# Two more blocks of the first projection in rounded products, and three low halves made by adding DMAs

## The reference

```python
h = _rmsnorm(x, norm_g[layer, 0]) * (1.0 + scale_m) + shift_m
proj = h @ w_in                        # (256 x 1024) @ (1024 x 3072)
a_val, a_gate, q, k, v, g = split(proj)
a = a_val * sigmoid(a_gate)            # then a convolution of 31 taps over the tokens
a = silu(layernorm(conv(a)))
r = silu(g) * head_rmsnorm(retention(rotary(q), rotary(k), v))
mix = concatenate([a, r]) @ w_out
```

## Time and profile before

| | before |
|---|---|
| median of 3 runs | 1171.31 us (1170.61 to 1175.93) |
| profiled execution, span | 1171.0 us (no other time is shown for this execution) |
| TensorE busy | 1112.6 us, 95% |
| VectorE busy | 816.0 us, 70% |
| ScalarE busy | 557.7 us, 48% |
| chain that ended last | TensorE 78%, VectorE 10%, DMA 5%, ScalarE 5% |
| mean granted TensorE clock | 0.985 of full speed |

### The profile page before, as it was taken

The page is one execution under the profiler, slowest core; times in us unless marked ns, Lnnn a source line. Parts: engine busy times, 40 slices in busy tenths (PEclk is TensorE's granted clock), DMA queues, the critical chain, the costliest instruction groups (busy, mean ns, idle before and its releaser), DMA issues.

```text
span 1171.0 us, 22089 instructions
## 1 busy us (share of the span) xinstructions
PE 1112.6 (95%) x9466; PEld 995.9 (85%) x9466; DVE 816.0 (70%) x1390; ACT 557.7 (48%) x876; POOL 44.6 (4%) x71
## 2 busy tenths in 40 slices
PE   6899898999999997879999999999999999999998
PEld 4778686988888885469999999999988899988898
DVE  1599466877578674875666654478899966659955
ACT  3224633445111124554555543356568846467944
POOL 0010001000000000000000000000000000042000
PEclk8999999999999998999999999989989999999999
DMA  9887688899848957865355555525433345343342
GB/s 369 356 280 269 250 323 315 305 339 328 335 182 258 342 186 165 323 245 184 140 184 182 183 189 185 187 81 180 145 109 114 130 153 177 131 153 117 108 145 72
DMA packets 38290, 246.46 MB, mean 210 GB/s; under 512 B 4400, under 2 KB 5584, under 8 KB 9648
## 3 DMA queue, kind: packets, MB, share of 16 engines
q1 hardware_dynamic: 29072, 182.36, 45.7%
q0 software_dynamic: 6240, 43.94, 10.0%
q10 hardware_dynamic: 2880, 18.74, 3.9%
HBM read 225.24 MB, written 19.79 MB: 209 GB/s over the span
## 4 chain that ended last, share of the span: by engine, by line
PE 78%; DVE 10%; DMA 5%; ACT 5%; issue 2%; SPq 0%; ACTq 0%; DVEq 0%
PE ps L1452 16%; PE ps L1454 15%; PE ps L1456 15%; PE ps L1459 10%; PE ps L1555 4%; DMA ca_dram<-more 2%; PE ps L1648 1%; PE ps L1528 1%; PE ps L2083 1%; PE ps L1601 1%; PE ps L1539 1%; PE ps L1534 1%; DMA more<-in_ada_w 1%; DVE ring_rounded L2229 1%; DMA ada_more<-in_ada_w 1%
## 5 line engine op out<-in xcount | busy, mean ns | idle before, releaser
L1452 PE MATMUL ps<-sq_rounded,w_high_rounded 128*128 128x256 f32 x1184 | 341.6, 288 | 2.5 <-DVE mixT_rounded L2236 1.3
L1456 PE MATMUL ps<-sq_rounded,ring_rounded 128*128 128x256 f32 x1184 | 336.2, 284 | 0.0
L2229 DVE TENSOR_TENSOR ring_rounded<-ring,w_high_rounded 128x1024 fp32r<-128x1024 f32 x220 | 260.6, 1226 | 92.1 <-ACT w_high_rounded L844 91.8
L1454 PE MATMUL ps<-hT_rounded,w_high_rounded 128*128 128x256 f32 x992 | 282.1, 284 | 0.0
L844 ACT ACTIVATE w_high_rounded<-ring 128x1024 fp32r<-128x1024 f32 x220 | 219.8, 1049 | 67.0 <-PE ps L1456 66.3
L1452 PEld LDWEIGHTS ps<-sq_rounded,w_high_rounded 128*128 128x128 f32 x1184 | 228.5, 193 | 11.0 <-issue 6.7
L1456 PEld LDWEIGHTS ps<-sq_rounded,ring_rounded 128*128 128x128 f32 x1184 | 228.6, 193 | 0.0
L1454 PEld LDWEIGHTS ps<-hT_rounded,w_high_rounded 128*128 128x128 f32 x992 | 191.8, 193 | 0.1
L1452 PE MATMUL ps<-more_rounded,w_high_rounded 128*128 128x256 f32 x448 | 127.4, 284 | 0.4 <-issue 0.3
L1456 PE MATMUL ps<-more_rounded,ring_rounded 128*128 128x256 f32 x448 | 126.8, 283 | 0.0
L1459 PE MATMUL ps<-big,ring 128*128 128x256 f32 x544 | 121.0, 381 | 0.0
(11 more groups left out here) (426 smaller groups left out, 1640.3 us busy)
## 6 DMA issues: line engine op xcount, KB each, us to landing
ring<-in_blocks SPq DMA_DIRECT2D x139, 1024.0 KB, 4.9
ada_w<-in_ada_w POOLq DMA_DIRECT2D x27, 1024.0 KB, 7.7
ada_more<-in_ada_w POOLq DMA_DIRECT2D x13, 1024.0 KB, 7.6
we_dram<-we_t ACTq DMA_DIRECT2D x8, 1024.0 KB, 8.3
ca_dram<-more ACTq DMA_DIRECT2D x8, 1024.0 KB, 11.9
ring<-we_dram SPq DMA_DIRECT2D x8, 1024.0 KB, 5.5
ring<-ca_dram SPq DMA_DIRECT2D x8, 1024.0 KB, 6.8
big<-in_ada_w SPq DMA_DIRECT2D x4, 1024.0 KB, 10.9
```

Of the source, the lines that this page charges most:

```text
L1452: nc.tensor.matmul(out, high[:, k, columns], x_high, start=start, stop=False, skip_group_check=True)
L1454: nc.tensor.matmul(out, high[:, k, columns], x_low, start=False, stop=False, skip_group_check=True)
L1456: last = nc.tensor.matmul(out, low[:, k, columns], x_high, start=False, stop=stop, skip_group_check=True)
L2229: nc.vector.tensor_tensor(rounded(w), w, w_high[:, c % 2, ks], ALU.subtract)\
```

## The change

Blocks 5 and 7 become split blocks. For them and for block 8 the low half is no longer made by VectorE. ScalarE rounds the block into `w_high` and then overwrites the ring slot with the rounded negative of the block; POOL then issues a DMA that reads the same block from DRAM again and adds it to what lies in the slot, which leaves the low half. TensorE takes the two products with the high weights for the whole block first, waits for the adding DMA, and then takes the product with the low weights. POOL issues the three adds behind pieces 10, 11 and 13 of `ada_w`. ScalarE's rounding is called at new places: block 5 behind the first sigmoid, block 7 behind the second, block 8 behind the copies of unit 4. On VectorE `centre` comes ahead of the low half of block 11. `dq_here` is folded into `lam_here` (which now counts to 32), `positions_here` and `p_here` into `small_here` (48).

```diff
-W_IN_SPLIT = (8, 9, 10, 11)
+W_IN_SPLIT = (5, 7, 8, 9, 10, 11)
+ADD_BEHIND = {10: 5, 11: 7, 13: 8}
+LOW_BY_DMA = {"w_in": (5, 7, 8)}
...
+            if b - start in LOW_BY_DMA.get(name, ()):
+                added[b] = 1 + sum(place[a] % 2 == place[b] % 2 for a in added)
+                low[b] = 0
+                continue
...
+            def add_low(name, j):
+                b = first_block[name] + j
+                pool.wait_ge(w_high_ready, 2 * split_place[b] + 2)
+                pool.dma_start(rounded(ring[:, b % RING]).rearrange("p a b -> p (a b)"), dram["blocks"][laid_out[b]],
+                               accum_op=ALU.add).then_inc(w_low_added[split_place[b] % 2], 16)
...
                 pool.dma_start(ada_slots[slot].rearrange("p a b -> p (a b)"), dram["ada_w"][n]).then_inc(ada_here[slot], 16)
+                if n in ADD_BEHIND:
+                    add_low("w_in", ADD_BEHIND[n])
...
+                    if b in low_added:
+                        nc.scalar.activation(w_high[:, c % 2], ring[:, b % RING], ACT.Copy).then_inc(w_high_ready, 1)
+                        nc.scalar.activation(rounded(ring[:, b % RING]), ring[:, b % RING], ACT.Copy, scale=-1.0)\
+                            .then_inc(w_high_ready, 1)
...
                 for n in (*pieces_at("w_in", 2 * j), *pieces_at("w_in", 2 * j + 1)):
                     modulation_row(n)
+                round_to(first_block["w_in"] + (6, 8)[j])
...
+                if j == 0:
+                    round_to(first_block["w_in"] + 9)
...
+                if b in low_added:
+                    pe.wait_ge(w_high_ready, 2 * split_place[b] + 1)
+                    first = places[0][4]
+                    for k, out, columns, x, start, stop in places:
+                        ...
+                        for part in x:
+                            nc.tensor.matmul(out, high[:, k, columns], part, start=first, stop=False,
+                                             skip_group_check=True)
+                            first = False
+                    pe.wait_ge(w_low_added[split_place[b] % 2], 16 * low_added[b])
+                    for k, out, columns, x, start, stop in places:
+                        last = nc.tensor.matmul(out, low[:, k, columns], x[0], start=False, stop=stop,
+                                                skip_group_check=True)
...
             decayed(0)
             decayed(1)
+            centre()
             lower_to(first_block["w_in"] + 12)
-            centre()
```

More of the change, by code:

```diff
@@ L215, in split_plan @@
 def split_plan(plan, first_block):
-    order, place, low = [], {}, {}
+    order, place, low, added = [], {}, {}, {}
     starts = sorted((b, name) for name, b in first_block.items())
@@ L227, in split_plan @@
             order.append(b)
+            if b - start in LOW_BY_DMA.get(name, ()):
+                added[b] = 1 + sum(place[a] % 2 == place[b] % 2 for a in added)
+                low[b] = 0
+                continue
             counts[SPLIT_LO[name]] += 1
             low[b] = counts[SPLIT_LO[name]]
-    return order, place, low
+    return order, place, low, added
 def program(nc, dram, out):
     plan, first_block = weight_plan()
-    split_order, split_place, split_low = split_plan(plan, first_block)
+    split_order, split_place, split_low, low_added = split_plan(plan, first_block)
     laid_out = {b: i for i, b in enumerate(from_inputs(plan))}
@@ L341, in program @@
         w_low_vector = sem("w_low_vector")
+        w_low_added = [sem(f"w_low_added{i}") for i in range(2)]
         a_high = sem("a_high")
@@ L398, in program @@
         braw_here = sem("braw_here")
-        dq_here = sem("dq_here")
         c_here = sem("c_here")
@@ L436, in program @@
         small_here = sem("small_here")
-        positions_here = sem("positions_here")
-        p_here = sem("p_here")
         angle_ready = sem("angle_ready")
@@ L796, in _ @@
                 pool.dma_start(ada_slots[slot].rearrange("p a b -> p (a b)"), dram["ada_w"][n]).then_inc(ada_here[slot], 16)
+                if n in ADD_BEHIND:
+                    add_low("w_in", ADD_BEHIND[n])
                 if n == PIECES + 4:
                     pool.dma_start(s5_small[:, 20:23], dram["s5_lam"]).then_inc(lam_here, 16)
-                    pool.dma_start(s5_dq[:, :], dram["s5_dq"]).then_inc(dq_here, 16)
+                    pool.dma_start(s5_dq[:, :], dram["s5_dq"]).then_inc(lam_here, 16)
                 if n == PIECES + 16:
@@ L805, in _ @@
             pool.dma_start(ssm_small, dram["ssm_small"]).then_inc(small_here, 16)
-            pool.dma_start(positions, dram["positions"]).then_inc(positions_here, 16)
-            pool.dma_start(p_tiles, dram["p"]).then_inc(p_here, 16)
+            pool.dma_start(positions, dram["positions"]).then_inc(small_here, 16)
+            pool.dma_start(p_tiles, dram["p"]).then_inc(small_here, 16)
             for m in range(5):
@@ L841, in round_to @@
                         act.wait_ge(blocks_done, split_order[c - 2] + 1 if c >= 2 else TOGETHER)
-                    for half in range(2):
+                    if b in low_added:
+                        nc.scalar.activation(w_high[:, c % 2], ring[:, b % RING], ACT.Copy).then_inc(w_high_ready, 1)
+                        nc.scalar.activation(rounded(ring[:, b % RING]), ring[:, b % RING], ACT.Copy, scale=-1.0)\
+                            .then_inc(w_high_ready, 1)
+                    for half in range(2) if b not in low_added else ():
                         ks = slice(4 * half, 4 * half + 4)
@@ L988, in _ @@
             head(0)
-            act.wait_ge(lam_here, 16)
+            act.wait_ge(lam_here, 32)
             nc.scalar.activation(s5_dt, s5_logdt, ACT.Exp).then_inc(s5_fun, 1)
@@ L1187, in _ @@
             round_to(first_block["xbc"] + 1)
-            act.wait_ge(small_here, 16)
+            act.wait_ge(small_here, 48)
             nc.scalar.activation(rounded(dt_w_high), dt_w, ACT.Copy).then_inc(dt_w_rounded, 1)
@@ L1441, in block_products @@
                     pe.wait_ge(w_here[b % RING], here[b])
+                if b in low_added:
+                    pe.wait_ge(w_high_ready, 2 * split_place[b] + 1)
+                    first = places[0][4]
+                    for k, out, columns, x, start, stop in places:
+                        if arrived and columns.start == 0:
+                            arrived(k)
+                        for part in x:
[6 more added lines that the diff above has]
+                                                skip_group_check=True)
                 waited = 0
-                for k, out, columns, x, start, stop in places:
+                for k, out, columns, x, start, stop in places if b not in low_added else ():
                     if split and k // 4 == waited:
@@ L1481, in project_tokens @@
                     x_high, x_low = (rounded(x[:, :, :]) for x in lhs)
-                    for i in range(TT):
+                    if b in low_added:
+                        pe.wait_ge(w_high_ready, 2 * split_place[b] + 1)
+                        for i in range(TT):
+                            for k in range(KB):
+                                for x in (x_high, x_low):
+                                    nc.tensor.matmul(ps[:, i], x[:, k, P * i:P * i + P], high[:, k],
+                                                     start=(k == 0 and i == 0 and x is x_high), stop=False,
+                                                     skip_group_check=True)
+                        pe.wait_ge(w_low_added[split_place[b] % 2], 16 * low_added[b])
+                        for i in range(TT):
+                            for k in range(KB):
+                                last = nc.tensor.matmul(ps[:, i], x_high[:, k, P * i:P * i + P], low[:, k], start=False,
+                                                        stop=(k == KB - 1), skip_group_check=True)
+                    for i in range(TT) if b not in low_added else ():
                         for k in range(KB):
@@ L2011, in _ @@
                 if m == 0:
-                    pe.wait_ge(small_here, 16)
+                    pe.wait_ge(small_here, 48)
                     pe.wait_ge(dt_w_low, 1)
@@ L2073, in ple_weights @@
             def ple_weights(phase):
-                pe.wait_ge(p_here, 16)
+                pe.wait_ge(small_here, 48)
                 return start_block(phase, 0).rearrange("p a b -> p (a b)").rearrange("p (k n) -> p k n", k=PLE // P)
@@ L2224, in lower_to @@
                     b = split_order[c]
+                    split_next[0] += 1
+                    if b in low_added:
+                        continue
                     for half in range(2):
@@ L2230, in lower_to @@
                             .then_inc(w_low_vector, 1)
-                    split_next[0] += 1
             def lower_tiles(name, n, full, high):
@@ L2424, in s5_steps @@
             def s5_steps():
-                dve.wait_ge(lam_here, 16)
+                dve.wait_ge(lam_here, 32)
```

(6 more changed lines are left out.)

## The result

The changed kernel took 1184.9 us (median of 6 runs, 1180.20 to 1187.64), the kernel before, run beside it, 1171.5 us (6 runs, 1170.61 to 1175.93). The ratio is 1.0091, with a 95% interval of 1.0071 to 1.0111. The forecast was 1169.0 us, within 0.5% of the time before; the range ended at 1175.0.

What follows compares the result with a forecast made beforehand. TensorE, busy 95% of the span, was taken as the bound. Blocks 5 and 7 gave -2.3 us (-1.7 with wait bubbles), all else 0: span 1171.0 to 1168.7, plus 0.3, makes 1169.0 us; range 1166.8 to 1175.0.

Steps and rivals of the forecast that it cites:

- The gain: TensorE, blocks 5 and 7: split, each takes 5.95 us in place of 7.10, together 2.3 us less.
- How long an add takes: Adding DMAs for blocks 5, 7, 8: 10.2 us from issue to landing, range 6.0 to 16.9; at 10.2 all land early.
- rival B: POOL's queue: adds run one behind the other, TensorE waits before block 8's low pass, 14.3 us, 1183.3 us; chance 0.11.
- X: Time one add holds POOL's queue; above 9.8 us block 8's low half is late, at 16.9 by 14.3 us.
- block 7 lands at 59.5 + 6.0: Block 7's load: lands at 65.5 us, so ScalarE is through at 69.5 and the add out at 70.0.
- Rival D: ScalarE held at block 7's late load, unit 4's copies behind it: 5.9 us lost, 1174.9 us; chance 0.06.
- the swap of the centring: VectorE, centring ahead of block 11's low half: gains nothing, cost 0.
- the semaphores: Semaphores folded together: transfers behind one count are issued within 1.1 us of each other, cost 0.
- the bubbles of the extra wait: TensorE, between high and low passes of blocks 5, 7 and 8: taken as 0, at worst 0.2 us each, 0.6 in all.

Runs made afterwards that it cites:

- e1: The change with plain loads in place of its three adding DMAs, the addition left out; ratio 0.9987 to the kernel before.
- e8: The change without block 5's add: adds for blocks 7 and 8 only, block 5's low half by VectorE; ratio 0.9989 to the kernel before.
- e9: e8 measured again, in more rounds beside the kernel before and the change; ratio 0.9998 to the kernel before.
- e4: The change with 16 idle float32 products on TensorE between block 8's high and low passes; ratio 1.0056 to the kernel before.
- e6: The change without its new split blocks and adds, leaving the rounding's place, swap and semaphores; ratio 0.9979 to the kernel before.
- e11: The changed kernel measured again, beside the kernel before; ratio 1.0076 to the kernel before.
- e2: The change with adds for blocks 5 and 7 only, block 8's low half by VectorE; ratio 1.0061 to the kernel before.
- e5: The change with no adding DMA, VectorE making the low halves of blocks 5, 7 and 8; ratio 1.0049 to the kernel before.
- e7: The change with block 7's add only, behind piece 12; low halves of blocks 5 and 8 by VectorE; ratio 1.0010 to the kernel before.

## Why the prediction was wrong

*The gain was right.* Blocks 5, 7 and 8 start at 67.48, 82.54 and 89.48 us. This profile's block 2 starts 1.0 us earlier than before, so these are the forecast 68.49, 83.55 and 90.5, less 1.0. Up to the end of block 8's high passes at 93.58 the 2.3 us are there; e1, e8 and e9 show them through to the scores.

*The first step that failed is "How long an add takes".* The 10.2 us, at most 16.9, stood for the time of one add from issue to landing. Measured were 12.6, 8.0 and 19.4 us. In this profile's time the add of block 8 was to go out at 78.0 and to land 5.3 us early; it went out 3.25 us later and took 9.2 us longer, and 3.25 + 9.2 - 5.3 is the wait of 7.2 us to rounding. Of its 19.4 us 12.2 had passed when piece 13, issued ahead of it on POOL's queue, had landed. The price of an add in engine time was nearly right, 2.5 us for each of two reads against 5.1 measured; but it entered only as a part of one landing time, for an add alone. It had to be summed over the stretch: 48 us for 43.

The prediction had the DMA share of 0.87 and 0.88 in blocks 5 and 7 before it and used it only as an argument for rival B. It turned B down because X would have to be four times 2.5 us. But B had the place, the sign, the wait (TensorE before block 8's low pass) and the queue: POOL's transfers did land one behind the other. Its sum with the measured terms is 75.8 + 8.0 and 7.2 for the two adds + 9.7 for the pieces and small loads between them = 100.7. It needed an X above 9.8 because it let the queue start at 70.0 and gave the pieces 5.0 us. So the price came to 7.2 us where B had 14.3, at an X of 16.9.

*The second is "block 7 lands at 59.5 + 6.0".* That row was measured without an add in front. Rival D named this, with its point of decision at 11 us, and was given 0.06 since the add was due to land at 62; it landed at 64.5, and the load took 13.3 us. The Trainium skill's sentence cited there (DMA: Bandwidth & Descriptors, Issuing engines are not separate DMA queues) says that DMAs of all issuing engines run on the same 16 engines. The trace agrees: a load on SP's queue took more than twice its time behind a transfer that POOL had issued, and 6.0 us again without it (e8). D's price came by another way than it said. VectorE did stand 5.4 us for the copies of unit 4, but what ended last was POOL behind ScalarE, and the add of block 8 behind what POOL then let go. So it was D's start with B's end.

*What the sum had no term for* is what follows the wait: block 8's passes take 7.81 us in place of 5.95, and 1.6 us of that is the clock, by e4 against the change. So the stage comes to -2.32 + 7.16 + 1.86 = +6.70 us; measured is 67.93 - 61.22 = 6.71.

*Rightly taken as nothing:* the swap of the centring and the semaphores (e6, by its ratio and its part after the scores), and the bubbles of the extra wait in blocks 5 and 7 (block 7's 5.94 us).

*What stays open.* The profiled spans differ by 10.3 us: -1.0 in the opening, +6.7 in the stage, +4.7 after the scores, where the change moved only the centring and some semaphore counts. In the 13 profiles that last part took 1063.8 to 1071.3 us, 1064.3 and 1065.9 for the kernel before alone, 1069.0 and 1065.7 for the change; stretches of lower clock fall in other places each time. The timed ratio of the first session is 8.3 to 13.0 us, above the stage; that of e11, 5.6 to 12.2 us, holds it. Some 2 to 4 us of the medians are therefore not placed. Nor is what other runs lose outside the stage: by their intervals e2 is slower by 4.5 us or more (2.56 in the stage), e5 by 2.7 or more (0.97), and e7 gains 0.6 at most (1.30). No run shows whether the low clock makes these differences. For the same reason the gain of e8 and e9, 2.3 us or 0.2%, is not shown in the time of the whole program. Only e6 has an interval wholly below 1, by 0.0001 and without a gain in its stage; no version here is shown to be faster than before.

The full engines and the late start of POOL's queue are not parted either: e1 relieves both, e8 takes one add away and starts the queue on time. That the adds cause the stall is shown; how late three adds would be with block 7's load on time is not.

## What to carry to other kernels

Before a stretch gets more transfers, sum the DMA engines' time in it, share times length, and add each new transfer at its own price; a landing time read from a row holds only for the traffic that was there, ahead of it on its own queue and beside it on the others. Then ask which load now stands behind the new transfer, which engine waits for that load, and what that engine's own issues release all at once. A wait in the middle of a TensorE block costs its length and, where the clock falls, the slow products behind it.

## What was not expected of the hardware

- A DMA that adds into on-chip memory took 5.1 us of all 16 engines for 1 MB, a plain load of the same block 2.6 us.
- POOL's issue of the adds took 0.87 to 0.89 us, and of plain pieces right behind one 0.86 to 0.88, against 0.53 for a piece alone; these records overlap, since the next starts 0.53 to 0.55 us after.
- During 7.2 us without products the granted clock fell to its lower level and stayed there for the following low pass; with idle products in the wait it stayed at 1.00.
- With the engines full, the order of issue decided which of several transfers was late (block 8's add or piece 13). What POOL had issued landed in the order of issue: 83.8, 87.7, 93.5 and 100.7 us in the change.
